# Rests written over the raw weights: seven raw places and six rounded ones instead of three and five

## The reference

```python
for i in range(DEPTH):                     # DEPTH = 4, kinds A, B, C, A
    ... = split_cols(x @ w_in[...], ...)   # attention of that kind, and over a memory
    mixed = jnp.concatenate([mix, mo], -1) @ w_out[i]
    x = layer_norm(ALPHA * x + mixed, ln1_g[i], ln1_b[i])
    x = layer_norm(ALPHA * x + swiglu(x, w_gate_up[i], w_down[i]), ln2_g[i], ln2_b[i])
for layer in range(DEPTH_2):               # DEPTH_2 = 2
    mod = c_act @ w_ada + b_ada            # c_act is one row
    ...                                    # rms_norm, proj = h @ w_in, two mixers, @ w_out
```

## Time and profile before

| | us |
|---|---|
| median of 3 runs | 1617.9 (1617.35 to 1620.54) |
| the profiled execution | 1618.14 |
| its span | 1616.3 |
| PE busy in the span | 1585.5 (98%) |
| DVE busy | 1064.7 (66%) |
| ACT busy | 728.6 (45%) |
| POOL busy | 48.9 (3%) |

### The profile page before, as it was taken

The page is one execution under the profiler, slowest core; times in us unless marked ns, Lnnn a source line. Parts: engine busy times, 40 slices in busy tenths (PEclk is TensorE's granted clock), DMA queues, the critical chain, the costliest instruction groups (busy, mean ns, idle before and its releaser), DMA issues. The chain is left out here.

```text
span 1616.3 us, 20190 instructions
## 1 busy us (share of the span) xinstructions
PE 1585.5 (98%) x8406; PEld 1326.7 (82%) x8406; DVE 1064.7 (66%) x1394; ACT 728.6 (45%) x877; POOL 48.9 (3%) x89
## 2 busy tenths in 40 slices
PE   8999999999999999999999999999999999999997
PEld 6998888888878888888888888788888878887986
DVE  7684766747666775675767656857767577556744
ACT  5445444443444444444444443454443334544452
POOL 2000000000000000000000000000100000000000
PEclk9999999999999999999999999999999999999999
DMA  8651466655425766362466744424766536333530
GB/s 304 225 200 62 169 238 232 251 215 182 158 79 173 283 244 250 132 230 81 153 251 234 263 179 163 158 77 150 269 241 240 228 131 240 132 131 117 209 118 26
DMA packets 45179, 299.89 MB, mean 186 GB/s; under 512 B 5460, under 2 KB 5716, under 8 KB 11552
## 3 DMA queue, kind: packets, MB, share of 16 engines
q1 hardware_dynamic: 38880, 278.48, 46.6%
q0 software_dynamic: 5776, 19.01, 3.5%
q10 hardware_dynamic: 432, 1.11, 0.2%
HBM read 296.20 MB, written 2.65 MB: 185 GB/s over the span
## 5 line engine op out<-in xcount | busy, mean ns | idle before, releaser
L945 PE MATMUL psum<-w_high,xt_high 128*128 128x512 f32 (+2 forms) x1472 | 575.2, 391 | 11.4 <-ACT arena L1300 4.5
L1447 DVE TENSOR_TENSOR w_low<-w_raw,w_high 128x2048 fp32r<-128x2048 f32 (+1 forms) x240 | 544.3, 2271 | 50.8 <-ACT w_high L1274 49.9
L947 PE MATMUL psum<-w_high,xt_low 128*128 128x512 f32 (+2 forms) x1472 | 565.2, 384 | 0.0
L946 PE MATMUL psum<-w_low,xt_high 128*128 128x512 f32 (+2 forms) x1472 | 564.1, 383 | 0.0
L1274 ACT ACTIVATE w_high<-w_raw 128x2048 fp32r<-128x2048 f32 (+1 forms) x240 | 456.7, 1905 | 233.2 <-DMA w_raw<-in_weights 153.7
L945 PEld LDWEIGHTS psum<-w_high,xt_high 128*128 128x128 f32 x1472 | 277.9, 189 | 67.6 <-issue 7.0
L947 PEld LDWEIGHTS psum<-w_high,xt_low 128*128 128x128 f32 x1472 | 277.5, 188 | 55.8
L946 PEld LDWEIGHTS psum<-w_low,xt_high 128*128 128x128 f32 x1472 | 278.1, 189 | 51.1
L1741 DVE TENSOR_TENSOR arena<-arena,psum 128x256 f32<-128x256 f32 x88 | 37.0, 421 | 206.4 <-ACT arena L1365 206.0
L945 PE MATMUL psum<-w_high,ht_high 128*128 128x512 f32 x352 | 140.8, 400 | 0.0
L947 PE MATMUL psum<-w_high,ht_low 128*128 128x512 f32 x352 | 137.5, 391 | 0.0
(11 more groups left out here) (229 smaller groups left out, 1610.6 us busy)
## 6 DMA issues: line engine op xcount, KB each, us to landing
w_raw<-in_weights SPq DMA_DIRECT2D x262, 1024.0 KB, 4.8
norm_params<-in_ln_g POOLq DMA_DIRECT2D x8, 512.0 KB, 4.2
norm_params<-in_ln_b POOLq DMA_DIRECT2D x8, 512.0 KB, 5.6
w_raw<-in_weights SPq DMA_DIRECT2D x4, 512.0 KB, 7.9
kv_outside<-arena POOLq DMA_DIRECT2D x3, 512.0 KB, 5.0
mem_kv<-kv_outside POOLq DMA_DIRECT2D x3, 512.0 KB, 3.5
norm_params<-mods_outside POOLq DMA_DIRECT2D x3, 512.0 KB, 6.0
x_rows<-in_x SPq DMA_DIRECT2D x2, 512.0 KB, 5.9
```

The source lines that it names most:

```text
L945: e.matmul(dst, a_hi, b_hi, start=first, stop=False)
L946: e.matmul(dst, a_hi, b_lo, start=False, stop=False)
L947: return e.matmul(dst, a_lo, b_hi, start=False, stop=last)
L1447: e.tensor_tensor(K.w_lo[:, s, 0:w], K.w_raw[:, r, 0:w], K.w_hi[:, s, 0:w].bitcast(F32), ALU.subtract).then_inc(K.taken.hit(t), 1)
```

## The change

`RAW` becomes 7 and `RING` 6. `w_low` has no memory of its own any more: it is laid over `w_raw`, with as many places, so a tile's rest replaces its raw weights in the same place. Three raw, five rounded and five rest places were 13 x 8 KiB for each partition; seven and six are 13 as well. A raw place is then free only when PE has done its last product on the tile (`used_up`, semaphore multiplied), or, for an ada tile, when DVE has summed it.

```diff
-RAW = 3
-RING = 5
+RAW = 7
+RING = 6
...
-        hi, lo = K.w_hi[:, s, :], K.w_lo[:, s, :]
+        hi, lo = K.w_hi[:, s, :], K.w_lo[:, j.tile % RAW, :]
...
-        e.tensor_tensor(K.w_lo[:, s, 0:w], K.w_raw[:, r, 0:w], K.w_hi[:, s, 0:w].bitcast(F32),
+        e.tensor_tensor(K.w_lo[:, r, 0:w], K.w_raw[:, r, 0:w], K.w_hi[:, s, 0:w].bitcast(F32),
...
         if t >= RAW:
-            sp.wait_ge(*K.halved(t - RAW, True))
+            sp.wait_ge(*K.used_up(t - RAW))
...
+        with ExitStack() as scope:
+            self.w_lo = scope.enter_context(nc.sbuf_tensor("w_low", [P, RAW, TW], F32R))
         self.w_raw = sb("w_raw", [P, RAW, TW])
         self.w_hi = sb("w_high", [P, RING, TW], F32R)
-        self.w_lo = sb("w_low", [P, RING, TW], F32R)
...
+    def used_up(self, t):
+
+        if self.plan.tiles[t].name == "w_ada_2":
+            return self.taken.at(t)
+        return self.multiplied.at((t, self.plan.last[t]))
```

## The result

| | before | after |
|---|---|---|
| median | 1618.15 us (4 runs, 1617.35 to 1620.54) | 1640.7 us (4 runs, 1637.45 to 1644.53) |
| ratio | | 1.0137, 95% interval 1.0117 to 1.0156 |
| span of the profiled execution | 1616.3 us | 1639.4 us |

The change costs 22.6 us. The forecast was 1625.7 us, with a range up to 1637: the sign was right, the loss three times as large as forecast.

The account below looks back on a forecast made before the run. PE's own work was taken to set the time. Terms -3.4 + 6.0 + 3.1 + 0.2 + 0.9 + 1.0 = +7.8 us; 1618.1 + 7.8 - 0.2 = 1625.7 us, own range 1622 to 1630, with 0.09 left above 1637.

Parts of the forecast that it names:

- Start: Kernel start: tiles 2 to 6 issued at once, tile 7 early, so PE's 4.10 us wait shrinks; 3.4 us gained.
- It can't be more than the 4.5 us of both such waits: Upper limit put on the gain at the start: PE's waits for ScalarE's evacuation (L1300), 4.5 us.
- rival 4: At the start: no gain, because POOL's norm gain comes late; 1629 us, chance 0.05.
- the backlog on SP's queue would not hold POOL's loads back: At the start: DMA engines go round queue rows packet by packet, so SP's longer backlog leaves POOL's loads undelayed.
- w_out to feed-forward: Between w_out and feed-forward in four layers: late rounding delays rests and residual, PE 1.5 us later each, 6.0 us lost.
- it lands at 194.5 us: Layer 0, w_out stretch: tile 28's transfer, free to issue at 189.66 us, lands 4.8 us later, the median.
- Borders between layers: Feed-forward to next layer, after layers 0 to 2: late landing delays turned rows or DVE's rest, 3.1 us lost together.
- Feed-forward steps: Steps with an ada tile: ACT waits 4.8 us, PE has 0.9 us in hand; one or two stalls, +1.0 us.
- Rival 1: Feed-forward steps break: landings mostly 6 us, each of 20 steps costs PE 0.3 us or more; to 1642 us, chance 0.13.
- After the last layer and in the second block: Landing 0.2 us late after the last layer, +0.2 us; between the second block's two layers PE 0.9 us later.
- stands at the next row block for xt_low: After the last layer: the 1.8 us wait for a rest goes, but PE then waits for xt_low, so nothing gained.
- for all but a few us: Whole span before the change: PE is busy for all but a few us of 1616.3 us.

## Why the prediction was wrong

**Start (-3.4 forecast, -2.9 measured).** The 4.10 us wait went, as worked out. Two things were missed, and nearly cancel. Before, PE's clock also stood low from 37.5 to 44.3 us, from within the stall on (0.56 and 0.58 in the two halves of 37 to 45), so the stall was worth more than its length. With the lists as before, the start gained 4.8 us in the records of one execution, 2.5 of it behind the stall, and 2.9 us in those of another, in which the clock fell at 34.6 us. "It can't be more than the 4.5 us of both such waits" was wrong, since it left the clock out. Against that, the backlog of transfers delayed POOL's norm gain: 14.2 us to its landing instead of 10.9, DVE waited 2.7 us for it, the rest of tile 4 began at 32.00 instead of 29.63 us and PE stood 2.79 us for it, with the clock low from 35.5 to 38.9 us. That was what rival 4 feared, in part. What the prediction drew from the Trainium skill, page "DMA: Bandwidth & Descriptors", section "Queues, rings and completion order", was that the backlog on SP's queue would not hold POOL's loads back. This conclusion, which the page itself doesn't draw, did not come true in this trace: with the backlog the norm's gain took 3.3 us longer to land.

**w_out to feed-forward (6.0 forecast, 16.4 measured).** This is the step that failed, and in it the term "it lands at 194.5 us", 4.8 us after issue. The mechanism and the place were right. So was the size where POOL's load was absent: 1.6 us lost in layer 3, and stalls of 1.50, 1.45 and 2.12 us in layers 0 to 2 with that load moved. The median of 262 transfers was applied to one that the change had made start together with another load. Before, that load fell into an empty stretch; I had not looked up what else is issued at the moment to which the transfer was moved. It made the landing 7.0 us in layer 0, 6.3 in layer 1 and 7.1 in layer 2, and the stalls 3.7, 2.9 and 3.8 us. In layers 0 and 2 the clock fell as well, for a further 2.7 and 1.6 us; the sum had no term for this.

**Borders between layers (3.1 forecast, 5.4 measured).** The waits for L1565 came, 1.0, 0.9 and 1.0 us long. Of the 4.0 us after layer 2, the clock has the larger part: it stood at the lower level from 1011.7 to 1018.4 us, from within a stall of 0.96 us on. With three idle products there it did not fall, and the border cost 1.5 us, the forecast figure. But it didn't fall there with POOL's load moved either, behind a stall of 1.01 us and without idle products, so this place alone doesn't show what they do. The border in the changed kernel, then with the load moved:

```profile
1010.00:1014.00 4.00, 3.04 (x21) 2.92 (x21) 3.93 (x7) 0.40 (x1) 1.19 (x3) 0.72 0.00 0
1014.00:1018.00 4.00, 4.00 (x11) 3.18 (x11) 2.67 (x5) 0.80 (x2) 0.46 (x1) 0.50 0.81 248
```

```profile
1005.00:1009.00 4.00, 2.99 (x22) 2.52 (x22) 4.00 (x5) 1.12 (x2) 1.52 (x3) 1.00 0.00 0
1009.00:1013.00 4.00, 4.00 (x19) 3.28 (x18) 2.33 (x5) 0.08 (x1) 0.12 (x1) 1.00 0.81 262
```


**Feed-forward steps (1.0 forecast, 1.5 measured).** Right, with 0.9 us in hand worked out and 1.1 us in the records (gate's product done at 272.96, PE on the bank at 274.03 us). One step of layer 3 broke, by 1.2 us. Rival 1 named about the measured time, 1642 us, but not its cause: twenty broken steps were its condition, and there was one.

**After the last layer and in the second block (0.2 and 0.9 forecast, 2.1 and 0.3 measured).** The wait for w_low (1.8 us) went and those for xt_low and L1798 took its place. That PE "stands at the next row block for xt_low" was right, but not that it ends there: the clock fell behind it, 1.5 us more.

**Sum.** The forecast is short by some 15 us: 10.4 at w_out, 2.3 at the borders, 1.9 after the last layer, 0.5 each at the start and in the steps, 0.4 in the products on the memory, less 0.6 in the second block. By cause, the idle products (in the w_out stretches of layers 0 to 2 and at the border to layer 3) gave back 6.5 us and the moved load 9.3 us, each to some 3 us; the two overlap, since with the load moved the clock didn't fall in layer 0 or at that border either (in layer 2 it still did, behind the stall of 2.12 us). One reading at the head of the prediction was loose as well: PE is not busy "for all but a few us", since 30.8 us of the span are not covered by its work, and three waits of over a us were left out of its list (L1730 twice, 1.4 and 1.2 us, and L1435, 1.2 us). They are the same in the changed kernel, so the sum doesn't change.

## What to carry to other kernels

More buffers don't allow earlier orders by themselves: with in-order engines, keep the list as it was and let the deeper buffer only move the transfers forward, then look whether a slot can be advanced. When an edit moves a transfer, list what else is issued on every DMA queue at its new moment; a median landing time, here, was that of a transfer alone. And give a new TensorE stall a price with a spread above its length, since the clock may fall with it: here the falls in layer 0, in layer 2 and behind it cost 2.7, 1.6 and 2.9 us on top, and stalls of 2.89 and 3.60 us had none.

## What the runs showed of the hardware

- Two loads issued together share the rate: 0.5 MB from POOL and 1 MB from SP, 3.5 and 4.8 us alone, took 7.0 us each when issued 0.3 us apart, with a second 1 MB transfer 3 us behind them. With the load 20 us later the 1 MB transfer took 4.9 us.
- PE's clock fell to its lower level in or just behind stalls of 3.66, 3.75 and 4.10 us, for up to 7 us, and products then follow each other in 0.43 us instead of 0.23. A stall of 3.60 us in the version with six raw places had no fall. A stall of 2.89 us in layer 1 had no fall behind it; one of 0.96 us after layer 2 had, and the same 2.81 us stall of layer 3 had a fall in one run of a version and none in another. The length of the stall alone doesn't tell. In none of the seven stalls that were given idle products did the clock fall, and the mean clock over all runs was higher with them (0.995 to 0.997 against 0.988 to 0.992). Runs of one and the same version differ by this: with the lists as before, the runs at a mean clock of 0.997 or more took 1611.0 to 1613.8 us, those at 0.994 took 1615.9 to 1616.4 us.
